# A transformer layer in f32 on one core: the products read and write their columns from last to first, and weights and activations start at other addresses

## What is computed

```python
hc = modulate(rms_norm(ctx, g_mix_pre), csh1, csc1)            # 256 x 2048
uf_c, xc_c, ug_c = mixer_inputs(hc, w_in, conv_w, conv_b)      # hc @ w_in (2048 x 3072)
hf_c, hb_c = bi_rglru(xc_c, *lru_p, None, None)
hx = modulate(rms_norm(x, g_mix_pre), sh1, sc1)                # 512 x 2048
uf_x, xc_x, ug_x = mixer_inputs(hx, w_in, conv_w, conv_b)
hf_x, hb_x = bi_rglru(xc_x, *lru_p, hf_c[:, -1], hb_c[:, 0])
y_x = mixer_output(uf_x, hf_x, hb_x, ug_x, w_fourier, b_fourier, w_out)   # 2-D DFT, 2048 x 2048
x = x + gt1 * rms_norm(y_x, g_mix_post)
hx2 = modulate(rms_norm(x, g_ffn_pre), sh2, sc2)
up = depthwise_conv(hx2 @ w_up, conv_ffn_w, conv_ffn_b, 1)     # 2048 x 11264
g, v = jnp.split(up, 2, axis=-1)
x = x + gt2 * rms_norm((gelu(g) * v) @ w_down, g_ffn_post)     # 5632 x 2048
```

## Time and profile before

| | |
|---|---|
| median of two runs | 2,105.55 us |
| the profiled execution, device time | 2,105.41 us |
| its span, first to last instruction | 2,103.6 us |
| PE (TensorE matmul) busy | 2,071.2 us, 11,682 instructions |
| DVE (VectorE) busy | 1,529.6 us |
| ACT (ScalarE) busy | 811.6 us |
| mean granted TensorE clock | 0.996 of full speed |
| moved by DMA | 311.19 MB, mean 148 GB/s |

### The profile page before, as it was taken

The page is one execution under the profiler, slowest core; times in us unless marked ns, Lnnn a source line. Parts: engine busy times, 40 slices in busy tenths (PEclk is TensorE's granted clock), DMA queues, the critical chain, the costliest instruction groups (busy, mean ns, idle before and its releaser), DMA issues.

```text
span 2103.6 us, 28297 instructions
## 1 busy us (share of the span) xinstructions
PE 2071.2 (98%) x11682; PEld 1772.5 (84%) x11682; DVE 1529.6 (73%) x2202; ACT 811.6 (39%) x1077; POOL 78.7 (4%) x145
## 2 busy tenths in 40 slices
PE   7999999999999999999999999999999999999998
PEld 4678887888777888888889898898988889888887
DVE  5567978876988975867767676676766758577577
ACT  5346577543323442423324233332333424233243
POOL 0000000001110000000000000000000000000002
PEclk9999999999999999999999999999999999999999
DMA  9953424434876523333333333334233333232343
GB/s 394 408 204 110 154 96 161 137 109 173 323 277 225 181 90 134 100 128 111 110 130 101 138 103 103 129 101 140 100 120 121 100 130 100 91 101 101 100 172 109
DMA packets 86193, 311.19 MB, mean 148 GB/s; under 512 B 9456, under 2 KB 13552, under 8 KB 84016
## 3 DMA queue, kind: packets, MB, share of 16 engines
q1 hardware_dynamic: 67824, 243.09, 32.7%
q0 software_dynamic: 17424, 65.50, 9.1%
q10 hardware_dynamic: 816, 0.79, 0.1%
HBM read 300.95 MB, written 8.39 MB: 147 GB/s over the span
## 4 chain that ended last, share of the span: by engine, by line
PE 80%; DVE 2%; ACT 1%; DMA 1%; issue 0%; DVEq 0%; ACTq 0%
PE bank L988 26%; PE bank L990 26%; PE bank L989 26%; DMA w_raw<-in_stream 1%; PE bank L1099 1%; DVE acc L2167 0%; PE bank L1284 0%; DVE w_lo L1532 0%; ACT w_hi L602 0%; PE bank L1313 0%; PE bank L1194 0%; DVE acc L2139 0%; ACT lru_u L698 0%; DVE cv L1544 0%; DVE x L2193 0%
## 5 line engine op out<-in xcount | busy, mean ns | idle before, releaser
L988 PE MATMUL bank<-h_hi,w_hi 128*128 128x512 f32 (+1 forms) x1968 | 711.2, 361 | 4.2 <-ACT y_lru L671 1.2
L989 PE MATMUL bank<-h_lo,w_hi 128*128 128x512 f32 (+1 forms) x1968 | 708.6, 360 | 0.0
L990 PE MATMUL bank<-h_hi,w_lo 128*128 128x512 f32 (+1 forms) x1968 | 707.2, 359 | 0.0
L1532 DVE TENSOR_TENSOR w_lo<-w_raw,w_hi 128x1024 fp32r<-128x1024 f32 x260 | 316.0, 1222 | 157.9 <-ACT w_hi L602 157.8
L988 PEld LDWEIGHTS bank<-h_hi,w_hi 128*128 128x128 f32 x1968 | 372.3, 189 | 63.6 <-issue 11.9
L602 ACT ACTIVATE w_hi<-w_raw 128x1024 fp32r<-128x1024 f32 x260 | 273.0, 1056 | 389.1 <-DMA w_raw<-in_stream 389.0
L990 PEld LDWEIGHTS bank<-h_hi,w_lo 128*128 128x128 f32 x1968 | 372.1, 189 | 56.6
L989 PEld LDWEIGHTS bank<-h_lo,w_hi 128*128 128x128 f32 x1968 | 372.3, 189 | 49.0
L988 PE MATMUL bank<-act_hi,w_hi 128*128 128x512 f32 (+1 forms) x688 | 265.0, 385 | 1.7 <-DVE acc L2139 1.5
L990 PE MATMUL bank<-act_hi,w_lo 128*128 128x512 f32 (+1 forms) x688 | 264.2, 384 | 0.0
L989 PE MATMUL bank<-act_lo,w_hi 128*128 128x512 f32 (+1 forms) x688 | 264.2, 384 | 0.0
(11 more groups left out here) (340 smaller groups left out, 2711.4 us busy)
## 6 DMA issues: line engine op xcount, KB each, us to landing
w_raw<-in_stream SPq DMA_DIRECT2D x340, 512.0 KB, 3.5
ada_raw<-in_adabg POOLq DMA_DIRECT2D x112, 512.0 KB, 4.3
ada_raw<-in_ada SPq DMA_DIRECT2D x64, 512.0 KB, 13.5
x<-in_x_t SPq DMA_DIRECT2D x4, 1024.0 KB, 8.4
acc<-in_adabg SPq DMA_DIRECT2D x8, 512.0 KB, 6.1
x<-in_x_t POOLq DMA_DIRECT2D x4, 1024.0 KB, 9.4
x_kept_d<-x SPq DMA_DIRECT2D x4, 1024.0 KB, 5.6
c<-in_ctx_t SPq DMA_DIRECT2D x2, 1024.0 KB, 14.3
```

Of the source, the lines that this page charges most:

```text
L988: t.matmul(out, w, v, start=start, stop=False)
L989: t.matmul(out, w, v_l, start=False, stop=False)
L990: return t.matmul(out, w_l, v, start=False, stop=stop)
L1532: v.tensor_tensor(lo_unit(n), raw_unit(n), hi_unit(n).bitcast(F32), ALU.subtract).then_inc(lo_done, 1)
```

## The change

`three` turns the order of the columns round in all its three matmuls, in the output and in the streamed operand alike; the weights are loaded as before. In front of `w_raw` 16 words (64 bytes) stay unused, so that the weights and all that lies behind them move up by 16 words, `h_hi` and `h_lo` do not. The unused words in front of `act_hi` shrink from 416 to 112, which puts `act` 304 words nearer to the weights, 288 words lower in all. `ada_rows` loses its own memory and takes the first half of `csq0`, which has the same 256 words.

```diff
@@ -189,6 +189,7 @@
         late_raw, h_hi = twice(ctx, "late_raw", "h_hi", [P, KT, L])
         x0, h_lo = twice(ctx, "x0", "h_lo", [P, KT, L])
+        sbuf(ctx, "gap_to_weights", [P, 16])
         w_raw, w_lo = twice(ctx, "w_raw", "w_lo", [P, RING, UNIT])
         w_hi = sbuf(ctx, "w_hi", [P, RING, UNIT], F32R)
@@ -220,7 +221,7 @@
                 pos0 = sbuf(s0, "pos0", [P, NPOS])
-                ada_rows = sbuf(s0, "ada_rows", [P, 2 * P])
+                ada_rows = csq0[:, 0, :]
                 ada0_raw = sbuf(s0, "ada0_raw", [P, A0SLOTS, 1024])
@@ -282,7 +283,7 @@
             cv = sbuf(s, "cv", [P, L])
-            sbuf(s, "gap_to_act", [P, 416])
+            sbuf(s, "gap_to_act", [P, 112])
             act_hi = sbuf(s, "act_hi", [P, CH, L], F32R)
@@ -648,7 +649,7 @@
-                a.activation(ada_rows[:, :], rows_bank(c)[:, 0:2 * P], ACT.Copy).then_inc(rows_copied, 1)
+                a.activation(ada_rows, rows_bank(c)[:, 0:2 * P], ACT.Copy).then_inc(rows_copied, 1)
@@ -985,6 +986,7 @@
             def three(out, w, w_l, v, v_l, start, stop):
 
+                out, v, v_l = out[:, ::-1], v[:, ::-1], v_l[:, ::-1]
                 t.matmul(out, w, v, start=start, stop=False)
                 t.matmul(out, w, v_l, start=False, stop=False)
                 return t.matmul(out, w_l, v, start=False, stop=stop)
```

## The result

The changed kernel takes 2,136.22 us (median; 2,133.30 to 2,139.14). Its ratio to the kernel before is 1.0146, with a 95% interval of 1.0086 to 1.0206. The profiled execution took 2,133.3 us around a span (first to last instruction) of 2,131.5, so the span grew by 27.9 us.

The account below looks back on a forecast made before the run. The prediction took PE's matmul-to-matmul distance to bound the kernel: 10,704 matmuls gaining 4.0 ns each, 43 us, bring the span from 2,103.6 to 2,060.6 us, so 2,062 us forecast; range 2,018 to 2,118.

Parts of the forecast that it names:

- Everything hangs on the distance, and other engines don't matter: PE's 10,704 matmuls of `three`: only their start-to-start distance counts, 13.3 ns beyond the columns each, 142 us in all.
- `ada_rows` costs 0, and no instruction is added: Copy at line 651, moved to `csq0`: no added wait, cost 0; reversed columns keep the same 10,704 matmuls.
- Walking against each other they pass and part. I take that as a gain.: Products of `three`: same-way column and weight streams lock, opposed ones part; 13.3 falls to 9.3 ns, gain 43 us.
- the lower end of 5.3 ns: Best single distances with weights from `sums1_hi`, 5.3 ns over the columns, taken as the gain's best end: 86 us, 2,020.
- The price is one of the weight load: Products of `three`: the next matmul's weight load disturbs the current column reads, making the 13.3 ns; argued, not shown.
- The new phases: Addresses modulo 128 words: weights 16 words on, `t` level, `h` 16 behind, `act` 304 lower to the weights; no separate size.
- The mixer: Mixer, 512- and 256-column products in turns: six starts should come from 1.05 us nearer 1.00.
- 2 (no change): Products of `three`: price fixed for each weight swap whatever the direction, or new phases settle alike; 2,105 us, chance 0.25.
- 4 (half the pace): Products of `three`: reversed access counts as scattered and runs at half the pace; about 3,900 us, chance 0.04.
- 3 (slower): Products of `three`: opposed streams collide more often, price 15 to 22 ns, 2,124 to 2,199 us; chance 0.15.
- upper end of 22 ns: Rival 3's highest price, from one 258-column matmul in the Fourier stage, about 22 ns over its columns: 2,199 us.
- The 2.5 ns and the reversed writes: Skill pages: warm matmul N/2.4 + 2.5 ns, matched by f32's 2.4 ns; non-contiguous PSUM patterns slow matmuls, read as not covering reversal.

## Why the prediction was wrong, step by step

- **Everything hangs on the distance, and other engines don't matter.** Right. The 11,682 instructions, the lengths on VectorE and ScalarE, the clock and the idle time stayed, and the distances alone give 37.2 - 3.9 = +33.3 us, of which 3.6 us went into idle time that is gone. The 13.3 ns are not fixed: right as well.
- **`ada_rows` costs 0, and no instruction is added.** The count bears out the second. Direction and offsets by themselves explain the account to 2 us, and no run took `ada_rows` apart, so its zero is not contradicted and not measured.
- **"Walking against each other they pass and part. I take that as a gain."** This is the step that failed. For the 6,288 matmuls with 512 columns the term has the wrong sign: not 13.3 to 9.3 ns but 14.1 to 20.0, +37 us instead of -25. For the 4,416 with 256 columns the sign was right and the size a quarter: -0.9 ns, not -4. The weakness was in the reading before it. The 13.3 ns that came back exactly in whole stages was taken for the mark of a bad lock. It is the mark of a favourable offset: of the 16 tried with 512 columns, only two give it, and the kernel before sat on one of them. Its trace held no 512-column matmul at another offset, so it had no row for that; the lower end of 5.3 ns came from single distances of 256-column matmuls and was carried over to 512 columns without one. For 256 columns the reading of the lock was not wrong: read upwards, offset 0 costs 13.2 ns, as much as nearly any of the 16, and most others cost less.
- **The price is one of the weight load.** Not borne out for 512 columns downwards: loads of 32, 64, 96 and 128 columns of weights give 20.0 ns alike. Upwards the load does matter for 512 columns, but not as a quantity: less of it costs more at offset 0 (13.8 ns for 128, 16.7 for 96 and 64, 18.3 for 32). For 256 columns upwards less of it costs less (6.7 ns for 64, 13.1 for 128), so there the reading may hold.
- **The new phases.** The prediction had `h` at 112 and `act` 304 words lower to the weights, and gave neither a price. Upwards they cost about 16 us on their own, the 512-column loss of 28.7 us less a gain of 12.6 with 256 columns. In the changed kernel the direction hides this.
- **The mixer.** Expected nearer 1.00 us for six, stayed at 1.05: where widths take turns, 15 ns are paid whichever way the columns are read.
- **The rivals.** 2 (no change) and 4 (half the pace) fall; 4 would have been 3,900 us. 3 (slower) gave 2,124 to 2,199 us, which holds the measured time, and its mark, six starts in 1.40 us, is what came. But its mechanism, columns that meet a weight load more often, should make the price smaller when the loads are shorter, and with 512 columns downwards it does not move. It was the right side for a reason that isn't borne out, and its price for 256 columns was wrong. Its upper end of 22 ns came from one single distance, the longest of that stretch; the mean of the 92 distances between `tok` products is 13.3 ns. A small slip beside it: the range begins at 2,018, and the gain at 5.3 ns, from which it is taken, gives 2,020.
- **The 2.5 ns and the reversed writes.** The Trainium skill, TensorE: Matmul & The Clock Gate, section Back-to-back issue gap, has 2.5 ns over the columns. It calls this the gap of an isolated matmul, and gives about 131 ns a matmul at 512 columns and about 81 ns at 128 for a stream with weight loads. Neither fits f32r here: with 256 columns or more the lowest group was 6.7 ns over and the highest 21.3, 512 columns took 226.7 ns at best and 128 columns 111.7. The prediction's agreement for plain f32 counts the columns of each record twice; line 1493 has 12 matmuls in the code and 24 records of 215.7 ns in the trace, so a plain f32 matmul of 256 columns takes four times its columns there. The Trainium skill, Advanced Engine Details and Errata, section Memory Cachelines, warns of non-contiguous PSUM patterns. Writing PSUM from last to first cost 0.0 ns here, so by the measurement that direction alone is no such pattern.

**What stays open.** The price of reading downwards is shown, and that neither the PSUM writes nor another engine nor the size of the load makes it. The mechanism inside PE is not shown: open is why 512 columns read downwards cost 20.0 ns and never less, what it is that repeats every 64 words upwards, and why a smaller load makes the upward price worse. 384 columns down cost 16.7 to 17.8 ns and 256 down 11.1 to 13.3, so the price grows with the columns, which rules out a fixed cost for each start; the runs say no more.

## What to carry to other kernels

When a run is nearly all matmuls, take the distance between their starts, by width and by tile, and treat a price that repeats exactly as possibly the best case before you disturb it: look for rows at other offsets, and if there are none, the sign is open. In a kernel like this, keep 512-column f32r products upwards, with columns and weights level modulo 64 words. An alignment or direction that helps one width may hurt another, so change them apart: moving weights, `t` and the sums of blocks 16 words on for the 256-column products alone won 0.4% (weights alone 0.15%), the new addresses for all lost 0.8%.

## What the runs showed of the hardware

- The distance of f32r matmuls with 512 columns read upwards depends on the offset of their columns to their weights: 13.3 to 21.3 ns over the columns, in groups that run with every other engine idle. Offsets 64 words apart gave the same price to 0.5 ns in the four pairs measured.
- Columns read from last to first: 20.0 ns over 512 columns, at each of twelve offsets and with four sizes of load. Written from last to first: nothing.
- Matmuls with 128 columns follow each other at 111.7 ns where their columns are 53.3 ns, up and down alike. So at that width it isn't the columns that set the distance; that it is the weight load is likely and wasn't tried.
- A sixth fewer weights loaded made the kernel 0.3% slower, 2,112.45 us in one run: 512 columns lost 2.6 ns a matmul, 256 columns gained 2.4.
- A plain f32 matmul of 256 columns takes two weight loads and two records of 215.7 ns each, four times its columns (line 1493).
